# Ranking the experts right behind the selection, loading the fourth place's number first, and refilling the fourth group expert by expert

## The reference

```python
s = sigmoid(t @ router_w)                      # 256 tokens x 64 experts
choice = s + router_bias                       # 4 of 8 groups by their top two, then the top 6 experts
w = s of the 6 chosen / their sum * 2.5        # gates
def expert_step(acc, p):                       # for each of the 64 experts
    hid = silu(t @ wg) * (t @ wu)              # wg, wu: 1024 x 256
    return acc + (hid @ wd) * g[:, None]       # wd: 256 x 1024
out = routed + (silu(t @ sh_w_gate) * (t @ sh_w_up)) @ sh_w_down
```

## Time and profile before

| | us |
|---|---|
| median of 3 runs (1241.38 to 1243.31) | 1242.99 |
| the profiled execution | 1242.61 |
| its span, first to last instruction | 1240.8 |
| PE busy | 1070.0 (86%) |
| DVE busy | 415.0 (33%) |
| ACT busy | 260.2 (21%) |
| SP's DMA queue (q1), share of 16 DMA engines | 87.1% |
| bytes moved | 445.54 MB |

### The profile page before, as it was taken

How to read it: one execution, slowest core, us unless ns; L and a number is a source line. 1 busy time by engine, 2 the same in 40 slices (tenths; PEclk the granted TensorE clock), 3 DMA queues, 4 the chain that set the end, 5 groups by cost and what they waited for, 6 DMA issues and landing times.

```text
span 1240.8 us, 19514 instructions
## 1 busy us (share of the span) xinstructions
PE 1070.0 (86%) x7694; PEld 649.5 (52%) x7694; DVE 415.0 (33%) x995; ACT 260.2 (21%) x622; POOL 84.1 (7%) x113
## 2 busy tenths in 40 slices
PE   8999998879887897577899999988899888886875
PEld 5784755353534454344688847554445353543442
DVE  3793623222413132221333327232233231321213
ACT  4382421111111101011132223211112111110110
POOL 3164000010000000000340000000100000000000
PEclk9999999989989999788999999999899899989888
DMA  9264699999999999999991545999999999999995
GB/s 364 88 266 175 272 404 419 421 421 394 420 412 421 421 420 420 420 421 416 345 342 35 208 199 237 371 420 421 419 378 422 422 421 421 420 421 420 420 420 205
DMA packets 83002, 445.54 MB, mean 359 GB/s; under 512 B 7886, under 2 KB 25357, under 8 KB 35292
## 3 DMA queue, kind: packets, MB, share of 16 engines
q1 hardware_dynamic: 80870, 439.25, 87.1%
q0 software_dynamic: 1616, 4.90, 1.1%
q10 hardware_dynamic: 422, 0.08, 0.0%
HBM read 443.12 MB, written 1.05 MB: 358 GB/s over the span
## 4 chain that ended last, share of the span: by engine, by line
PE 53%; DMA 37%; SPq 3%; issue 3%; DVE 2%; ACT 1%; POOL 0%; DVEq 0%
DMA ring<-in_l_exp_w_up 24%; PE bank L1171 11%; DMA ring<-in_l_exp_w_down 10%; PE bank L1329 8%; PE bank L1006 5%; PE bank L1364 4%; PE bank L934 4%; PE bank L1009 2%; PE bank L877 2%; DMA ring<-in_l_exp_w_gate 2%; PE bank L1077 2%; PE bank L1134 2%; SPq L677 2%; SPq L735 2%; PE bank L1209 1%
## 5 line engine op out<-in xcount | busy, mean ns | idle before, releaser
L1329 PE MATMUL bank<-ring,big 128*32 128x256 f32 x2816 | 184.4, 422 | 65.9 <-DMA ring<-in_l_exp_w_up 42.5
L1329 PEld LDWEIGHTS bank<-ring,big 128*32 128x32 f32 x2816 | 112.6, 121 | 133.8 <-issue 100.0
L1171 PE MATMUL bank<-ring,big 128*64 128x512 f32 x608 | 150.9, 631 | 25.0 <-DMA ring<-in_l_exp_w_up 25.0
L1171 PEld LDWEIGHTS bank<-ring,big 128*64 128x64 f32 x608 | 50.1, 145 | 115.6 <-issue 114.9
L1364 PE MATMUL bank<-ring,big 128*32 128x512 f32 (+1 forms) x736 | 90.2, 633 | 17.8 <-DMA ring<-in_l_exp_w_down 15.7
L1626 ACT ACTIVATE ys_high<-bank,gcol 128x512 fp32r<-128x512 f32 (+1 forms) x86 | 58.3, 678 | 158.3 <-PE bank L1364 101.0
L2219 DVE TENSOR_TENSOR mixT<-mixT,bank 128x512 f32<-128x512 f32 x120 | 79.8, 685 | 27.1 <-PE bank L1298 17.9
L1209 PE MATMUL bank<-pick,xs_high 128*128 128x128 f32 x352 | 83.1, 279 | 0.0
L2189 DVE TENSOR_TENSOR big<-big,bank 128x256 f32<-128x256 f32 x22 | 9.3, 422 | 220.0 <-PE bank L1329 220.0
L1209 PE MATMUL bank<-pick,xs_low 128*128 128x128 f32 x352 | 81.5, 275 | 0.0
L1209 PEld LDWEIGHTS bank<-pick,xs_high 128*128 128x128 f32 x352 | 67.7, 192 | 10.0 <-issue 9.8
(11 more groups left out here) (311 smaller groups left out, 1436.8 us busy)
## 6 DMA issues: line engine op xcount, KB each, us to landing
ring<-in_l_exp_w_gate SPq DMA_DIRECT2D x122, 1024.0 KB, 13.0
ring<-in_l_exp_w_up SPq DMA_DIRECT2D x122, 1024.0 KB, 17.5
ring<-in_l_exp_w_down SPq DMA_DIRECT2D x112, 1024.0 KB, 17.8
ring<-in_l_w_in SPq DMA_DIRECT2D x13, 1024.0 KB, 12.3
ring<-in_l_w_out SPq DMA_DIRECT2D x8, 1024.0 KB, 8.8
lead_par<-in_l_exp_w_down SPq DMA_DIRECT2D x6, 1024.0 KB, 12.0
ring<-in_l_exp_w_gate SPq DMA_DIRECT2D x8, 512.0 KB, 9.3
ring<-in_l_exp_w_up SPq DMA_DIRECT2D x8, 512.0 KB, 10.9
```

The lines of the kernel that those rows point to most:

```text
L1171: ins = mm(ps[SLOTS * q:SLOTS * q + SLOTS, :], xg[:, c, SLOTS * j:SLOTS * j + SLOTS], both[:, c, 0:n:n - 1], start=(c == 0), stop=(c == C ...
L1329: ins = mm(ps[r, 0:HID], xn[:, c, r], loop_weights(L, j, w)[:, c, :], start=(c == 0), stop=(c == C - 1))
```

## The change

Four things are changed, in both layers. VectorE does `rank_key` and `ranks` right behind the first `pick`, ahead of any copy of gathered tokens, and the gate values behind the last copy. TensorE runs `ranked` behind the fifth of the eight gathers and no longer inside `gate_up(0)`; VectorE writes `order` behind the copy of piece 5, and copies pieces 3, 5 and 7, while ScalarE copies 0, 1, 2, 4 and 6. SyncE loads the number of the fourth place (single0's fourth expert) alone, issues its gate weight, and only then loads all four. The last refill of the fourth group (turn0) goes pair by pair where it went by kind.

```diff
--- before.py
+++ after.py
@@ -79,6 +79,8 @@
 LED = BEGIN["turn0"]
 APART = 32768.0
 AHEAD = 5
+RANKED_BEHIND = 4
+DVE_FIRST = (3, 5, 7)
 
 NEG = -1e30
 SENT = -2e30
@@ -695,9 +697,11 @@
 
                 first, second, third, fourth = (ExpertLoop(L, kind, banks, S, bank, i=0) for kind in ALONE[:4])
                 sp.wait_ge(S("order"), L + 1)
-                experts = in_place(first.next_place())
+                at = first.next_place()
+                fourth_expert = sp.value_load(order[0:1, bass.ds(at + GE - 1, 1)], min_val=0, max_val=NE - 1)
                 sp.wait_ge(S("shared_gates"), L + 1)
-                into_place(experts, GE - 1, 0)
+                into_place([fourth_expert] * GE, GE - 1, 0)
+                experts = in_place(at)
                 sp.wait_ge(S("first_half"), L + 1)
                 for h in range(2):
                     if h:
@@ -718,7 +722,7 @@
                 refill(third, [GE + j for j in range(GE)], [piece for piece in PAIR_BY_PAIR if piece not in LEAD])
                 experts = in_place(fourth.next_place())
                 refill(third, experts, LEAD)
-                refill(fourth, experts, [piece for piece in BY_KIND if piece not in LEAD])
+                refill(fourth, experts, [piece for piece in PAIR_BY_PAIR if piece not in LEAD])
                 for kind in ALONE[4:]:
                     lp = ExpertLoop(L, kind, banks, S, bank, i=0)
                     refill(lp, in_place(lp.next_place()))
@@ -1170,8 +1174,6 @@
                             both = both.rearrange("p (w c f) -> p c w f", w=n, c=C)
                             ins = mm(ps[SLOTS * q:SLOTS * q + SLOTS, :], xg[:, c, SLOTS * j:SLOTS * j + SLOTS],
                                      both[:, c, 0:n:n - 1], start=(c == 0), stop=(c == C - 1))
-                        if lp.kind == "first" and pr == 0 and c == 1:
-                            ranked(lp)
                         if lp.kind == "first" and pr == 0 and c == C // 2 - 1:
                             ins.then_inc(S("first_half"), 1)
                     lp.made(ins, ("gu", pr))
@@ -1247,8 +1249,11 @@
                     if lp.kind == "first":
                         for c in range(C):
                             bank_made(gather(c, bank_open(pe, ("gather", L, c))), ("gather", L, c))
+                            if c == RANKED_BEHIND:
+                                ranked(lp)
                         gate_up(lp, 0)
                         shared_gate_up(0, 1, 1, AHEAD)
+                        pe.wait_ge(lp.sem("pick"), lp.count(2, 2, 0))
                         ps = lp.open(pe, "rowsT")
                         for tb in range(TB):
                             ins = flip(ps[:, P * tb:P * tb + P], routed[:, tb, :, :].rearrange("p a b -> p (a b)"), ident[:])
@@ -1686,8 +1691,9 @@
                     for key, a, b in LAST_PARTS if last else [(("dn", h), HALF * h, HALF * h + HALF) for h in range(2)]:
                         high(lp, key, 0, a, b)
 
-                for c in range(0, C, 2):
-                    gathered(bank_read, bank_done, ("gather", L, c))
+                for c in range(C):
+                    if c not in DVE_FIRST:
+                        gathered(bank_read, bank_done, ("gather", L, c))
                 alone_groups(L, wide, narrow)
                 lp = ExpertLoop(L, "narrow", banks, S, bank)
                 run_groups(act, lp, narrow, LATE - 1)
@@ -2025,7 +2031,7 @@
                 ps = bank_read(dve, ("pos", L))
                 link(v.tensor_tensor(posm, exr[:, :, 0:NE], ps[:, 0:TB * NE].rearrange("p (a e) -> p a e", a=TB), ALU.add))
 
-                def gates_and_ranks():
+                def gate_values():
 
                     link(v.tensor_reduce(norm[:, 0:2], cho, AX.X, ALU.add))
                     link(v.reciprocal(norm[:, 2:4], norm[:, 0:2]))
@@ -2033,6 +2039,9 @@
                         ins = v.tensor_scalar(gates[:, tb, :], cho[:, tb, :], norm[:, 2 + tb:3 + tb], SCALE,
                                               ALU.mult, ALU.mult)
                     link(ins)
+
+                def rank_keys():
+
                     dve.wait_ge(S("consts"), 12)
                     ps = bank[banks.at[("pos", L)][0]]
                     ins = v.scalar_tensor_tensor(rank_key, ps[:, TB * NE:3 * NE], float(NE), prior[:], ALU.mult, ALU.add)
@@ -2091,8 +2100,6 @@
                     ps = lp.read(dve, "ranked")
                     v.tensor_copy(order[0:1, :], ps[0:1, 0:NE]).then_inc(S("order"), 1)
                     lp.done(v.tensor_tensor(over_cap[0:1], ps[0:1, P:P + NE], filled[0:1], ALU.subtract), "ranked")
-                    v.memset(in_turn[:, :, 0, NE:], FAR)
-                    v.memset(in_turn[:, :, 1, NE:], 0.0)
 
                 def sorted_rows(lp):
 
@@ -2116,7 +2123,8 @@
                 def wide(lp, ahead=None):
 
                     if lp.kind == "first":
-                        ordered(lp)
+                        v.memset(in_turn[:, :, 0, NE:], FAR)
+                        v.memset(in_turn[:, :, 1, NE:], 0.0)
                         shared_hidden(0)
                     lp.read(dve, "gT")
                     if lp.kind != "first":
@@ -2261,14 +2269,17 @@
 
                 def first_gathered():
 
-                    gates_and_ranks()
+                    rank_keys()
+                    ranks()
+                    for c in DVE_FIRST:
+                        gathered(bank_read, bank_done, ("gather", L, c))
+                        if c == RANKED_BEHIND + 1:
+                            ordered(first)
+                    gate_values()
                     link(v.memset(st[:], 0.0))
-                    for c in range(1, C, 2):
-                        if c == 5:
-                            ranks()
-                        gathered(bank_read, bank_done, ("gather", L, c))
-
-                select(ExpertLoop(L, "first", banks, S, bank, i=0), "wide", 0, 1, first_gathered)
+
+                first = ExpertLoop(L, "first", banks, S, bank, i=0)
+                select(first, "wide", 0, 1, first_gathered)
                 dve.wait_ge(S("acc_begun"), TB * (L + 1))
                 alone_groups(L, wide, narrow)
                 dve.wait_ge(S("rounds"), L + 1)
```

## The result

The changed kernel took 1244.18 us (median of 20 runs) against 1242.75 us for the kernel before on the same chip (20 runs). The ratio is 1.0019, 95% interval 1.0011 to 1.0027: about 2.4 us slower, between 1.4 and 3.4, which is within 0.2% and at its edge; the two medians lie 1.43 us apart. One of the changed kernel's 20 executions took 3639.39 us and is left out of the ratio. The forecast was 1245.0 with a range of 1240.3 to 1247.8, and +2.0 us for the difference. Profiled, the span went from 1240.8 to 1244.0 us and the mean granted TensorE clock from 0.949 to 0.944 of full speed.

The account below looks back on a forecast made before the run. Within a MoE the DMA queue, at about 420 GB/s, was taken as the bound, so empty queue time counts. Start -0.4 plus refill +2.4 gave +2.0 us, 1245.0 on the median, range 1240.3 to 1247.8.

Parts of the forecast that it names:

- The start: Start of each MoE: earlier list and first transfer gain 0.2 us per layer, -0.4 in all; bounds 0 and 3.5 per layer.
- the fixed issues: SyncE's issues at 162.72 and 174.28 wait for TensorE and stay unmoved; the 3.5 us lead shrinks there to 0.2.
- With no gap: Queue before back1: full when ups 0 and 1 are issued, the same 44 MiB passed by 263.6, last up at 265.4.
- One sign that I would be wrong: Downs of single0: the prediction is wrong if they are used over 1 us earlier than 196.0.
- the last up of turn0's refill lands at another time: Second sign of being wrong: the last up of turn0's refill lands at a time other than 265.4.
- the early load arrives whole: Rival at the MoE start: issues at 162.72 and 174.28 move along, both layers gain 3.5 us; 1238.4, chance 0.14.
- The refill: Turn0's refill and back1: gate 3 lands 5 us later, queue runs empty; 1.9 and 0.5 lost, +2.4 us, bounds -1.4 and +3.8.
- the gate stage stays warm: Rival at back1's gate stage: the clock holds or returns at once, refill gives 0.0 and -1.4; 1241.2, chance 0.16.
- Cold throughout: Rival at back1's gate stage: cold throughout with the queue empty for it; 1246.4 to 1248.8, say 1247.5, chance 0.25.
- used up: Queue behind back1's refill: the later emptiness of the kernel before, 1.8 us in layer 0, takes back part of the loss.

Follow-up runs that it names:

- start_only: The changed kernel with the old refill of turn0, by kind: 1241.8 us, ratio 1.0004 to the kernel before.
- start_held: Changed start with the old refill, the first transfer held back until the first half of `gate_up(0)` is read: 1241.32 us, ratio 0.9999 to the kernel before.
- warm_gate: The changed kernel with 8 filler matmuls ahead of back1's gate stage: 1240.14 us, ratio 0.9988 to the kernel before.
- refill_only: The kernel before with only turn0's last refill changed, to pair by pair: 1242.57 us, ratio 1.0018.
- refill_between: The kernel before with one up put ahead of the last two gates in the fourth group's refill: 1238.87 us, ratio 0.9986.
- warm_up: The kernel before with 9 filler matmuls ahead of back1's up stage: 1237.68 us, ratio 0.9971.
- between_warm: The kernel before with one up ahead of the refill's last two gates and 7 fillers ahead of back1's up stage: 1238.56 us, ratio 0.9970.
- between_start: The changed kernel with only one up ahead of the last two gates in the refill, no filler: 1239.36 us, ratio 0.9983 to the kernel before.
- warm_three: The kernel before with fillers ahead of back1's up stage (9), turn0's `gate_up(1)` (7) and single0's downs (8): 1238.43 us, ratio 0.9977.
- warm_three_start: Changed start with the old refill, fillers ahead of back1's ups, turn0's `gate_up(1)` and single0's downs: 1239.20 us, ratio 0.9977 to the kernel before.

## Why the prediction was right, and where not

**The start: worth nothing, as said, but not in the way that was said.** -0.4 us was forecast, bounds 0 and 3.5 per layer. The list came about where it was put (145.6 less the 1.16 us of the earlier `pick` is 144.44; its row ends at 144.67), the first transfer 0.4 us late (145.24; 145.67), the halves in time (148.74; 148.82), and the issues at 162.7 and 174.3 stayed. start_only (1.0004) and start_held (0.9999) can't tell -0.4 from nothing. That the fixed issues take the lead away holds. That it turns into empty queue holds for the smaller part: by the DMA share the engines worked 2.8 and 1.2 us longer for the same bytes. "With no gap" in the queue behind the start missed that the rate then stays at 410 GB/s for 40 us in layer 0 (start_only 412, start_held 421), about 1 us. One sign that I would be wrong was that single0's downs are used over 1 us earlier; they moved the other way, from 55.19 to 56.27 us behind `pick`, with the stage colder (6.04 for 5.34). Another was that the last up of turn0's refill lands at another time. In the changed kernel no stage waits for it, but where one does, it comes in layer 0 at 126.4 in start_only and 127.3 in warm_gate, against 124.6 in the kernel before; in layer 1 start_only has 124.6 too.

The Trainium skill, "DMA: Bandwidth & Descriptors", "Rules for kernel authors", advises to issue a DMA early. Here that gained nothing, since later issues wait for TensorE to free units: the rival "the early load arrives whole" (1238.4) is out.

**The refill: mechanism and size right.** 2.4 us were forecast; refill_only measured 1.8 permille, 2.2 us (0.9 to 3.6). Its trace has the steps of the sum within 0.7 us, in us behind `pick` for layers 0 and 1: the gate stage begins at 120.01 and 119.64 (said: 119.55 and 119.49), and the next gates are issued at 125.26 and 125.82 (said: 125.25 and 125.2). Behind gate 3's landing, at 257.78, it moved another 1.27 MB, 3.0 us at the full rate (said: 3.2), and its windows around back1 show 1.7 and 0.9 us more lost queue time than the kernel before (said: 1.9 and 0.5). Gate 3 itself moved by 5.3 us in layer 0 (114.69 to 120.01), where 5.0 were said. The gate stage was put at 5.6 us; from its start to the issue behind it it is 5.25 and 6.2 there, and 5.7 in layer 0 of the changed kernel.

**The term that was mis-sized: what the two changes do together in layer 0.** In the changed kernel layer 0's gate stage begins at 122.23 and the next gates are issued at 127.94, 2.2 and 2.7 us later than with the refill alone. Warm_gate, with the same start and refill, begins its gate stage at 122.46; in layer 1 the delay of the changed kernel against refill_only is 0.8. I had given the new start no effect on what comes behind it. About 1 us of the delay is the slower queue behind the early transfer; the rest is open. What I gave as loss, 1.9 and 0.5, reads in the windows around back1 as 3.1 and 1.3 us, and with the rest 6.3 us in both layers. From layer 0's `pick` to layer 1's the profile grew by 3.4 us (625.36 to 628.78), from there to the end by 0.9; the span grew by 3.2 and the time by the ratio by about 2.4. One profile of each kernel is no better than that, and I can't say where the rest is taken back.

**The clock.** Of the rivals, "the gate stage stays warm" (1241.2) is refuted by 8.96 and 9.50 us for both stages. Its price was about right: 1.8 us less than the kernel before were said, and warm_gate's ratio makes it 1.5. "Cold throughout" (1247.5) did not come: the clock was granted 0.50 up to 265 and 1.00 from 266, 4 us into the stage. The Trainium skill, "TensorE: Matmul & The Clock Gate", "HAM oscillation — how this bites in real kernels", has a burst behind a DMA wait start cold; the rows of these stages agree with that, and not with its case of a whole burst cold (7.3 us here). Not each wait does so: refill_between's up stage in layer 0 came warm out of 3.77 us.

**What the sum held without naming it.** The change moves coldness from the up stage to the gate stage, and both orders pay for one cold stage per layer. The end of the old one stands in the sum only as the 1.8 and 3.1 us of emptiness that are "used up". warm_up shows where these come from: with the up stage warm the rate around back1 rises from 402 and 391 GB/s to 412 and 410, 3.2 us in two layers, and the ratio makes it 3.6, because the ups' end releases the next transfers too. The refill term has earned its size. The near hit of the whole is in part luck: the start's loss in layer 0 was not foreseen, and the time shows less of it than the profile.

**Open.** Why between_warm and between_start have cold gate stages behind waits of 3.4 to 4.5 us and lose nothing is read from windows; a queue lengthened without moving the gate was not tried. And warm_gate against warm_up leaves the split of the 2.2 us between clock and delay uncertain. Why an early first transfer slows the queue behind it is open too.

## What to carry to other kernels

Where a queue of transfers is the bound and each refill waits for a stage, count two things for each order: how many transfers lie behind the last one that the next stage needs, and how long that stage takes at the clock it will have after its wait. Queue time must cover stage time; one transfer moved past two others turned a gain of 1.4 to 1.7 permille into a loss of 1.8 to 1.9. An earlier first transfer was worth nothing here, where the later issues are tied to a compute engine that is already busy without a break.

## What the runs showed of the hardware

The same wait can leave the stage behind it warm or cold. In refill_between a wait of 3.77 us was followed by 3.66 us in layer 0, one of 3.78 by 6.21 in layer 1; in warm_three and warm_three_start 2.03 and 2.05 us were followed by 5.35 and 3.66. So a trace of one execution does not tell what a given wait will cost in a changed kernel, and the 1.3 to 2.6 us that a stage of 3.66 us lost here when it began cold is the grain of a forecast. Filler matmuls in the wait brought the full clock where they reached to within 0.6 us of the stage (warm_up, both layers); where 2 us were left, both layers of warm_three were cold and both of warm_three_start warm.

The same DMA share can move fewer bytes: in layer 0, 40 to 80 us behind `pick`, start_only moved 412 GB/s at a share of 1.00 and start_held 421 at 1.01, with only the place of one 1 MiB transfer 3 us apart.
